# Block compression without paired columns, and the output gate of the delta-rule heads moved into the attention stage

## The chip, the cores and the metric

The kernel runs on one core of a Trainium2 chip. The metric is the device time of one execution in microseconds (us), where lower is better. The engines of the core are TensorE (PE; its weight loads are shown apart as PEld), VectorE (DVE), ScalarE (ACT), GpSimd (POOL) and SyncE (SP, which issues the DMAs). Each engine runs its own list of instructions in order and waits on semaphores that the others raise.

## What is computed

A decoder trunk of two layers on 512 tokens of width 1024, in float32. In each layer three groups of token mixers read the same normalised input: gated DeltaNet (4 heads of 64), sparse attention (8 query heads of 64 and 2 key/value heads, with a compressed, a selected and a window branch), and a short gated convolution. Then come an output projection and a SwiGLU feed-forward network. The change touches two parts of the reference:

```python
def compress_blocks(t, pe, w1, w2):
    nb = T // CMP_STRIDE                                   # 512 / 16
    blk = t.reshape(b, nb, CMP_STRIDE, g, d)
    win = jnp.concatenate([blk[:, :-1], blk[:, 1:]], axis=2) + pe[:, None, :]
    flat = win.transpose(0, 1, 3, 2, 4).reshape(b, nb - 1, g, CMP_LEN * d)
    return jax.nn.gelu(flat @ w1) @ w2                     # for keys and for values

o_gdn = rms_norm(o_gdn, gdn_norm[l]) * jax.nn.silu(heads(gz))
```

## The kernel before

**One layer on PE.** The input projection runs in 34 groups, numbered n = 0 to 33 (`GROUPS`); each is one PSUM bank filled in three passes (high and low parts of both operands, `three_pass`, L514). Other work is placed by hand between groups, by n, in the same order on every engine. After it come transposes of queries and keys, the attention stage, the output projection and the feed-forward network. The weights are fetched by SP, copied to `w_hi` by ACT (`split_hi`, L962), and `w_lo` is formed by POOL (`split_lo`, L1223).

**Compression.** Behind group 20 `cmp_first` (L553) multiplies `w1c` with the windows in `x2`: 32 float32 matmuls that the trace shows as 64 records. Those of the keys (k = 0) write PSUM partitions 0 to 63 and those of the values (k = 1) partitions 64 to 127, in turn, so that they use the two column halves of the array. The position term `pe` is not added to the data. It stands as two more window columns behind the 31 of each head (`NW1 = NC + 2`), copied into `x2` by ACT (L989). DVE's `cmp_hidden` (L1394 to L1403) adds it and does the GELU with a Tanh of ACT (L1046). Behind group 21 PE runs `cmp_second` (L563), DVE runs `cmp_norm` (L1407 to L1416, with the product of L1411), and behind group 23 PE runs `cmp_third` (L570).

**Gate of the delta-rule heads.** `z` holds the gate's input. At n = 9 ACT computes its Tanh (L1068), between the Tanh of beta (L1065) and the exponentials of the decay (L1069 to L1075), which DVE turns into `g` (L1451). PE's cumulative sum (L596) and POOL's `make_trig` wait for `g`. Later, between `one_minus(0)` (L1243) and `split_lo(10)`, POOL turns `z` into silu(z) times the norm gain (L1289, L1290, L1291) and raises `zgate`.

**Hops.** From n = 24 on, `hop` (L623, L662, L666) puts chains of dependent small matmuls between the passes. `hop_dve` and `hop_act` copy each result for the next one. DVE also normalises keys there (`k_norm`, L1503 and L1504, both inputs in SBUF).

**Attention.** 64 items (unit and query tile) run in ticks 0 to 75. In tick s: PE computes `scores(s)` (L754, L755), DVE its row maximum (L1682, L1679), ACT the exponential (L1135), DVE the reciprocal of the sum (L1688, in the next tick), and POOL scales the probabilities (`scale_probs`, L1315). PE transposes them three ticks later (`p_transpose(s)`, L771, in tick s + 3), DVE and ACT copy that to SBUF, and `pv` (L785) and `cmp_pv` (L793) follow. Two score tiles are issued together in each tick divisible by four. I call the scaling of item s scale(s) and its transposes ptr(s).

**The tail of the delta rule** lies in the same ticks, from OG_TICK = 41 on. ACT squares `og` (41), DVE sums (tick 42, L1720) and makes the inverse root by a seed and three Newton steps (tick 43, ten small operations, L1724 and L257 to L261). POOL has one piece per tick in ticks 45 to 52 ahead of its scaling: for each of four token tiles one product with the root (L1323) and one with the gate (L1326). PE transposes the two halves (`gdn_out`, L823) in ticks 54 and 56, and ACT and DVE split each into high and low (L977, L1729). The second of them waits until the first has been split.

Of the kernel before, what the change touches and what calls it, by code (L numbers as in the profile page):

```python
# [41 lines left out]
class Semaphores(dict):  # L42
# [22 lines left out]
    "norm_gains": 32, "oS": 4, "rb": 1, "rbps": 1, "rstd1": 1, "oall": 1, "og": 4, "ogT": 2, "ored": 1, "oroot": 1, "osq": 1, "pTa": 32, "pTd": 32,  # L65
# [4 lines left out]
    "x_res": 16, "zgate": 1, "zth": 1,  # L70
# [15 lines left out]
def trunk(nc, A, out):  # L86
# [7 lines left out]
    NW1 = NC + 2  # L94
# [31 lines left out]
    with ExitStack() as ctx:  # L126
        def sb(name, shape, dt=F32):
# [21 lines left out]
                      sb(f"kg{l}", [P, 3, HEAD]), sb(f"pe_c{l}", [P, 2, 16]), sb(f"w2c{l}", [P, HEAD]))  # L149
# [5 lines left out]
        peb = sb("peb", [P, 2])  # L155
# [34 lines left out]
        XW = T + CMP_LEN  # L190
        x2 = at(0, 2, 2, XW)
# [6 lines left out]
        hid = at(10240, 3, 2 * NC)  # L198
# [75 lines left out]
        def load_params(sp, l):  # L274
# [5 lines left out]
            def row(name, n):  # L280
# [4 lines left out]
                (p.w2c[:], A["nsa_cmp_w2"][l].rearrange("k i d -> (k i) d")),  # L285
# [180 lines left out]
        def tensor_layer(pe, l):  # L466
# [351 lines left out]
            def gdn_out(m):  # L818
                pe.wait_ge(*S.at("og", NT, l))
# [6 lines left out]
            for tick in range(N_ITEMS + LAG_PV):  # L826
# [14 lines left out]
                if tick in (OG_TICK + 13, OG_TICK + 15):  # L841
                    gdn_out((tick - OG_TICK - 13) // 2)
# [104 lines left out]
        def scalar_layer(act, l):  # L947
# [31 lines left out]
            def empty_group(n):  # L979
# [49 lines left out]
            for n in range(len(GROUPS)):  # L1029
# [33 lines left out]
                if n == 9:  # L1063
# [3 lines left out]
                    act.wait_ge(*S.at("gtr", 6, l))  # L1067
                    nc.scalar.activation(zt, z, ACT.Tanh, scale=0.5).then_inc(S["zth"], 1)  # L1068
# [80 lines left out]
            for tick in range(N_ITEMS + LAG_PV):  # L1149
# [24 lines left out]
                if tick in (OG_TICK + 14, OG_TICK + 16):  # L1174
                    m = (tick - OG_TICK - 14) // 2
# [38 lines left out]
        def pool_layer(pool, chain, l):  # L1214
# [38 lines left out]
            if l == 0:  # L1253
# [603 lines left out]
```

## Time and profile before

| | |
|---|---|
| median of 3 runs | 1549.39 us (1548.87 to 1550.99) |
| the profiled execution | 1548.87 us, its span 1546.8 us |
| PE busy | 1436.6 us, 93% of the span |
| DVE, POOL, ACT busy | 683.1, 645.1, 512.8 us |
| mean granted clock of PE | 0.971 of full speed |
| chain that ended last | PE 76%, DVE 13%, issue 4%, ACT 3%, POOL 2% |

The span is the time from the first to the last instruction; the execution's own time is 2.07 us longer. Times in rows count from the start of the span. The first layer's stages lie at about 29 to 226 us (input projection), 226 to 258 (queries and keys), 258 to 365 (attention) and 365 to 772 (output projection and feed-forward). The second layer repeats them about 768 us later. The clock is given as a share of full speed, so that 1.00 is 2.4 GHz and 0.5 is 1.2 GHz.

### The profile page before, as it was taken

The numbers are of one execution on the slowest core, as the hardware profiler recorded it, in microseconds if no ns is written. First come the engines' busy times: TensorE is split into PE (matmuls) and PEld (weight loads), VectorE is DVE, ScalarE is ACT, GpSimd is POOL, SyncE is SP. The second block draws the span as 40 slices with busy tenths as digits, with TensorE's granted clock in tenths as the row PEclk, the third lists the DMA queues.
The fourth block names the chain that finished last, engine by engine and source line by source line (L and its number), as shares of the span: only waits on it lengthen the run. The fifth ranks groups of instructions, "written<-read, shape, count | busy, mean of one in ns | idle before, by whom it ended". The sixth has DMA issues, their size and how long they took to land.

```text
span 1546.8 us, 19725 instructions
## 1 busy us (share of the span) xinstructions
PE 1436.6 (93%) x8050; PEld 1199.0 (78%) x8050; DVE 683.1 (44%) x1208; ACT 512.8 (33%) x888; POOL 645.1 (42%) x371
## 2 busy tenths in 40 slices
PE   5998986979999999999978989879799999999999
PEld 4887875647988888888868888756489888888887
DVE  6527467663334402433164284576623443033421
ACT  5453215452332312232235423154434232123220
POOL 4375332453343433434423833333433443443432
PEclk9999998999999999999989999979999999999999
DMA  6214120001533233233222341200022333333332
GB/s 170 85 57 106 50 55 1 1 1 44 98 84 108 77 102 109 82 109 93 84 76 64 80 105 28 55 1 1 1 56 82 106 85 102 101 84 109 83 101 75
DMA packets 182857, 112.64 MB, mean 73 GB/s; under 512 B 46576, under 2 KB 170480, under 8 KB 182768
## 3 DMA queue, kind: packets, MB, share of 16 engines
q1 hardware_dynamic: 182768, 111.39, 25.9%
q8 instruction: 64, 1.05, 0.3%
q14 instruction: 25, 0.20, 0.0%
HBM read 108.49 MB, written 2.88 MB: 72 GB/s over the span
## 4 chain that ended last, share of the span: by engine, by line
PE 76%; DVE 13%; issue 4%; ACT 3%; POOL 2%; DMA 1%; SPq 1%; ACTq 0%; DVEq 0%; POOLq 0%
PE ps L514 62%; PE ps L623 2%; PE ps L785 2%; PE ps L771 2%; DVE arena L1487 2%; DVE st L260 1%; DVE att L1682 1%; PE ps L754 1%; PE ps L755 1%; DVE arena L1495 1%; DVE hT_hi L1647 1%; DVE arena L271 1%; ACT hT_lo L977 1%; POOL w_lo L1223 1%; PE ps L469 1%
## 5 line engine op out<-in xcount | busy, mean ns | idle before, releaser
L1223 POOL TENSOR_TENSOR w_lo<-w_raw,w_hi 128x2048 fp32r<-128x2048 f32 (+1 forms) x100 | 453.5, 4535 | 628.9 <-ACT w_hi L962 628.9
L962 ACT ACTIVATE w_hi<-w_raw 128x2048 fp32r<-128x2048 f32 (+1 forms) x100 | 188.6, 1886 | 571.3 <-PE ps L514 570.9
L514 PE MATMUL ps<-hT_hi,w_lo 128*128 128x512 f32 x928 | 232.9, 393 | 0.0
L514 PE MATMUL ps<-hT_hi,w_hi 128*128 128x512 f32 x912 | 228.6, 392 | 0.4 <-DVE hT_lo L1364 0.4
L514 PE MATMUL ps<-hT_lo,w_hi 128*128 128x512 f32 x912 | 226.9, 390 | 0.0
L514 PEld LDWEIGHTS ps<-hT_hi,w_lo 128*128 128x128 f32 x928 | 175.6, 190 | 36.5
L514 PEld LDWEIGHTS ps<-hT_lo,w_hi 128*128 128x128 f32 x912 | 170.6, 188 | 35.6 <-issue 0.3
L514 PEld LDWEIGHTS ps<-hT_hi,w_hi 128*128 128x128 f32 x912 | 169.3, 188 | 36.2 <-DVE hT_lo L1364 1.3
L1729 DVE TENSOR_TENSOR aT_lo<-ffn_tmp,aT_hi 128x512 fp32r<-128x512 f32 x44 | 142.2, 3231 | 30.8 <-ACT aT_hi L977 30.8
L1784 DVE TENSOR_TENSOR ffn_tmp<-ps,ffn_tmp 128x512 f32<-128x512 f32 x44 | 30.4, 692 | 243.6 <-ACT ffn_tmp L1201 243.6
L514 PE MATMUL ps<-w_hi,aT_hi 128*128 128x512 f32 (+1 forms) x608 | 132.9, 345 | 0.0
L514 PE MATMUL ps<-w_lo,aT_hi 128*128 128x512 f32 (+1 forms) x608 | 132.3, 344 | 0.0
L514 PE MATMUL ps<-w_hi,aT_lo 128*128 128x512 f32 (+1 forms) x608 | 131.9, 344 | 0.0
L977 ACT ACTIVATE arena<-ps 128x512 f32<-128x512 f32 (+4 forms) x146 | 69.8, 494 | 179.1 <-PE ps L623 87.1
L514 PEld LDWEIGHTS ps<-w_hi,aT_hi 128*128 128x128 f32 x608 | 98.7, 188 | 15.4 <-issue 0.8
L514 PEld LDWEIGHTS ps<-w_hi,aT_lo 128*128 128x128 f32 x608 | 98.8, 188 | 14.5
L514 PEld LDWEIGHTS ps<-w_lo,aT_hi 128*128 128x128 f32 x608 | 98.8, 188 | 14.2
L1793 DVE SCALAR_TENSOR_TENSOR x_tok<-ps,st,x_tok 128x512 f32<-128x512 f32 x32 | 24.0, 750 | 189.1 <-PE ps L514 189.1
L623 PE MATMUL ps<-arena 128*128 128x128 f32 x512 | 71.7, 291 | 15.3 <-DVE arena L1552 6.9
L623 PEld LDWEIGHTS ps<-arena 128*128 128x128 f32 x512 | 65.4, 201 | 19.8 <-DVE arena L1552 7.8
L1315 POOL TENSOR_SCALAR arena<-arena,att,ngt 128x512 f32<-128x512 f32 (+3 forms) x80 | 51.5, 647 | 56.4 <-DVE att L1688 55.4
L754 PE MATMUL ps<-hT_lo,hT_hi 128*128 128x256 f32 (+2 forms) x128 | 58.2, 455 | 10.2 <-DVE hT_hi L1647 10.2
(283 smaller groups left out, 1836.6 us busy)
## 6 DMA issues: line engine op xcount, KB each, us to landing
w_raw<-in_w_gate_up SPq DMA_DIRECT2D x88, 512.0 KB, 5.1
w_raw<-in_w_in SPq DMA_DIRECT2D x20, 1024.0 KB, 5.4
w_raw<-in_w_down SPq DMA_DIRECT2D x16, 1024.0 KB, 5.1
w_raw<-in_w_out SPq DMA_DIRECT2D x32, 256.0 KB, 4.5
w_raw<-in_w_down SPq DMA_DIRECT2D x8, 768.0 KB, 4.5
w_raw<-in_w_in SPq DMA_DIRECT2D x2, 1120.0 KB, 5.8
w_raw<-in_w_in SPq DMA_DIRECT2D x2, 1056.0 KB, 6.3
x_tok<-in_x SPq DMA_DIRECT2D x4, 512.0 KB, 5.4
```

Of the source, the lines that this page charges most:

```text
L514: mm = nc.tensor.matmul(out_ap, a(ab, k), b(bb, k), start=first and i == 0, stop=last and i == len(kts) - 1)
L623: mm = nc.tensor.matmul(ps[:, bank, h * P:(h + 1) * P], lhs(h), rhs(h), start=True, stop=True)
L754: nc.tensor.matmul(o, q_ap, kst[:, br * 2 + g, 0:n], start=True, stop=False, skip_group_check=True)
L771: mm = nc.tensor.transpose(ps[:, 4 + s % 2, j * P:(j + 1) * P], prob[u % 2][i][:, j * P:(j + 1) * P], ident[:])
L785: nc.tensor.matmul(ps[rows, PV_BANK[p % 2], j * P:T], kv[:, j, v0:v0 + HEAD], pT[(2 * v + g) % 4][:, j * T:j * T + T - j * P], start=br == ...
L962: nc.scalar.activation(whi[:, c % 2, 0:kt * w], raw[:, c % 2, 0:kt * w], ACT.Copy).then_inc(S["w_hi"], 1)
L977: return nc.scalar.activation(dst, src, ACT.Copy)
L1223: nc.gpsimd.tensor_tensor(wlo[:, c % 2, 0:kt * w], raw[:, c % 2, 0:kt * w], whi[:, c % 2, 0:kt * w].bitcast(F32), ALU.subtract).then_inc(S ...
L1315: nc.gpsimd.tensor_scalar(prob[u % 2][i], prob[u % 2][i], att[:, 1, s % 8:s % 8 + 1], ngt[:, i, 3 * h + 1 + br:3 * h + 2 + br], ALU.mult, ...
L1487: chain(V.tensor_tensor(tmp, a, d, ALU.mult))
L1729: V.tensor_tensor(dst, full, hi.bitcast(F32), ALU.subtract).then_inc(done, 1)
L1784: V.tensor_tensor(ft[:, 2 + cnt % 2, :], ps[:, 2 * (i % 2) + 1, :], ft[:, cnt % 2, :], ALU.mult).then_inc(S["up_mul"], 1)
```

## The change

`cmp_first` no longer pairs keys with values. All its matmuls write partitions 0 to 63, first the 16 of the keys, then those of the values. The position term leaves `x2`. It is computed by 16 further matmuls for each k whose moving operand is one column of `pe_c`. `cmp_hidden` and `cmp_second` follow that layout: 64 partitions with keys and values side by side.

```diff
-                for m in range(16):
-                    for k in range(2):
-                        mm = nc.tensor.matmul(ps[k * HEAD:(k + 1) * HEAD, 3, 0:2 * NW1].rearrange("p (g n) -> p g n", g=2),
-                                              w1c[:, k, m, :], x2[:, k, :, 2 * m:2 * m + CMP_STRIDE * (NW1 - 1) + 1:CMP_STRIDE],
-                                              start=m == 0, stop=m == 15, skip_group_check=True)
+                for k in range(2):
+                    for m in range(16):
+                        nc.tensor.matmul(ps[0:HEAD, 3, k * P:k * P + 2 * NC].rearrange("p (g n) -> p g n", g=2),
+                                         w1c[:, k, m, :], x2[:, k, :, 2 * m:2 * m + CMP_STRIDE * (NC - 1) + 1:CMP_STRIDE],
+                                         start=(k == 0 and m == 0), stop=(m == 15), skip_group_check=True)
+                    for m in range(16):
+                        mm = nc.tensor.matmul(ps[0:HEAD, 3, k * P + 2 * NC:k * P + 2 * NC + 1], w1c[:, k, m, :],
+                                              prm[l].pe_c[:, k, m:m + 1], start=False, stop=(m == 15), skip_group_check=True)
...
-                    ev(x2[:, g, :, T:XW:2], prm[l].pe_c[:, g, :].rearrange("p (o m) -> p o m", o=1).broadcast_to([P, 2, 16]))
...
-                chain(V.tensor_copy(peb[:, 0:1], ps[:, 3, NW1 - 1:NW1]))
-                chain(V.tensor_scalar(hid[:, 0, :].rearrange("p (g n) -> p g n", g=2),
-                                      ps[:, 3, 0:2 * NW1].rearrange("p (g n) -> p g n", g=2)[:, :, 0:NC], peb[:, 0:1], None, ALU.add))
+                for k in range(2):
+                    chain(V.tensor_copy(peb[:, k:k + 1], ps[0:HEAD, 3, k * P + 2 * NC:k * P + 2 * NC + 1]))
+                for k in range(2):
+                    cols = slice(k * 2 * NC, (k + 1) * 2 * NC)
+                    chain(V.tensor_scalar(hid[:, 0, cols], ps[0:HEAD, 3, k * P:k * P + 2 * NC], peb[:, k:k + 1], None, ALU.add))
```

The gate's Tanh moves from n = 9 to tick 43 on ACT, and POOL's three gate operations leave the projection (with `zgate`, for which DVE waited at the groups of `cx`). In the attention POOL takes the Newton steps over from DVE, which keeps the seed. The pieces become 16 of 128x256, two per tick in ticks 44 to 47, one per tick in ticks 49 to 56, with a pass over `zt` in tick 48. `gdn_out` moves from ticks 54 and 56 to 58 and 60, and so do the splits of its results.

```diff
-                    act.wait_ge(*S.at("gtr", 6, l))
-                    nc.scalar.activation(zt, z, ACT.Tanh, scale=0.5).then_inc(S["zth"], 1)
...
+                if tick == OG_TICK + 2:
+                    act.wait_ge(*S.at("ored", 1, l))
+                    nc.scalar.activation(zt, z, ACT.Tanh, scale=0.5).then_inc(S["zth"], 1)
...
-            pool.wait_ge(*S.at("zth", 1, l))
-            chain(nc.gpsimd.tensor_scalar(zt, zt, 0.5, 0.5, ALU.mult, ALU.add))
-            chain(nc.gpsimd.tensor_tensor(z, z, zt, ALU.mult))
-            nc.gpsimd.tensor_tensor(z.rearrange("p t (h d) -> p (t h) d", d=HEAD), z.rearrange("p t (h d) -> p (t h) d", d=HEAD),
-                                    prm[l].gng[:].rearrange("p (o d) -> p o d", o=1).broadcast_to([P, NT * GH, HEAD]), ALU.mult
-                                    ).then_inc(S["zgate"], 1)
...
-                if tick == OG_TICK + 4:
-                    pool.wait_ge(*S.at("oroot", 1, l))
-                if OG_TICK + 4 <= tick < OG_TICK + 12:
-                    gdn_piece(tick - OG_TICK - 4)
+                if tick == OG_TICK + 2:
+                    pool.wait_ge(*S.at("oseed", 1, l))
+                    newton(st[:, 2, 0:16], st[:, 1, 0:16], st[:, 3, 0:16])
+                if OG_TICK + 3 <= tick < OG_TICK + 7:
+                    gdn_piece(2 * (tick - OG_TICK - 3))
+                    gdn_piece(2 * (tick - OG_TICK - 3) + 1)
+                if tick == OG_TICK + 7:
+                    pool.wait_ge(*S.at("zth", 1, l))
+                    chain(nc.gpsimd.tensor_scalar(zt, zt, 0.5, 0.5, ALU.mult, ALU.add))
+                if OG_TICK + 8 <= tick < OG_TICK + 16:
+                    gdn_piece(tick - OG_TICK)
                 scale_probs(tick)
...
-                    rsqrt(chain, st[:, 2, 0:16], st[:, 1, 0:16], st[:, 3, 0:16])
-                    dve.nop().then_inc(S["oroot"], 1)
+                    V.tensor_scalar(st[:, 2, 0:16].bitcast(I32), st[:, 1, 0:16].bitcast(I32), -0.5, RSQRT_SEED,
+                                    ALU.mult, ALU.add).then_inc(S["oseed"], 1)
...
-                if tick in (OG_TICK + 13, OG_TICK + 15):
-                    gdn_out((tick - OG_TICK - 13) // 2)
+                if tick in (OG_TICK + 17, OG_TICK + 19):
+                    gdn_out((tick - OG_TICK - 17) // 2)
```

## Rows read from the trace of the kernel before

**Rows 1.** The page: busy time, share of the span and instructions.

```profile
PE 1436.6 (93%) x8050; PEld 1199.0 (78%) x8050; DVE 683.1 (44%) x1208; ACT 512.8 (33%) x888; POOL 645.1 (42%) x371
```

**Rows 2.** Windows: length, busy (instructions) of PE, PEld, DVE, ACT, POOL; clock, DMA, GB/s.

```profile
325.00:344.00 19.00, 13.57 (x84) 9.01 (x84) 13.23 (x38) 9.55 (x36) 12.78 (x21) 0.91 0.00 1
...
365.00:772.00 407.00, 406.79 (x1992) 343.84 (x1991) 129.26 (x117) 108.76 (x110) 165.34 (x38) 1.00 0.34 94
...
346.00:350.10 4.10, 4.10 (x13) 1.10 (x11) 0.16 (x1) 1.15 (x5) 1.19 (x2) 0.58 0.00 0
```

**Rows 3.** Timeline at the decay's exponentials: start, length, engine, line, operation, [wait before].

```profile
75.44 1.04 ACT L1068 ACTIVATE arena<-arena 128x1024 f32<-128x1024 f32 x1
76.50 1.28 ACT L1069 ACT_TABLE_LOAD   x1
...
80.11 0.40 PE L596 MATMUL ps<-gsc,tri 128*128 128x16 f32 x2 [4.00 <-DVE gsc L1451]
```

**Rows 4.** Timeline at the compression.

```profile
130.35 4.07 PE L553 MATMUL ps<-arena 128*64 128x66 f32 x64
...
140.27 0.22 DVE L1399 TENSOR_TENSOR arena<-arena 128x62 f32<-128x62 f32 x1
...
141.33 0.42 PE L563 MATMUL ps<-w2c,arena 64*31 64x64 f32 x8 [1.24 <-DVE arena L1403]
...
142.67 4.62 POOL L1223 TENSOR_TENSOR w_lo<-w_raw,w_hi 128x2048 fp32r<-128x2048 f32 x1 [9.04 <-ACT w_hi L962]
143.11 4.32 DVE L1411 TENSOR_TENSOR arena<-arena 31x128 f32<-31x128 f32 x1
...
150.33 0.24 PE L570 MATMUL ps<-ident,arena 31*128 31x31 f32 x1 [2.64 <-DVE arena L1416]
```

**Rows 5.** Timeline: two short float32 batches of a hop on PE.

```profile
169.12 1.10 PE L662 MATMUL ps<-arena 128*128 128x64 f32 x8 [0.87 <-ACT arena L977]
...
170.16 0.66 PE L666 MATMUL ps<-arena 128*64 128x128 f32 x8
```

**Rows 6.** Timeline at POOL's gate operations, among the hops.

```profile
159.45 1.49 POOL L1289 TENSOR_SCALAR arena<-arena 128x1024 f32<-128x1024 f32 x1
...
160.06 1.42 DVE L1504 TENSOR_TENSOR arena<-arena,kg 128x512 f32<-128x512 f32 x1
...
161.02 2.68 POOL L1290 TENSOR_TENSOR arena<-arena 128x1024 f32<-128x1024 f32 x1
...
162.25 1.16 PE L623 MATMUL ps<-arena 128*128 128x128 f32 x8 [1.27 <-DVE arena L1550]
...
166.74 0.69 DVE L1504 TENSOR_TENSOR arena<-arena,kg 128x512 f32<-128x512 f32 x1
```

**Rows 7.** Timeline: POOL's Newton steps for the queries, first and last of 12 operations.

```profile
204.13 0.24 POOL L1247 TENSOR_TENSOR st<-st 128x32 f32<-128x32 f32 x1
...
207.66 0.25 POOL L1250 TENSOR_TENSOR st<-st 128x32 f32<-128x32 f32 x1
```

**Rows 8.** Timeline of POOL in the attention: scale(42), two pieces, scale(56).

```profile
324.56 0.66 POOL L1315 TENSOR_SCALAR pbuf<-pbuf,att,ngt 128x384 f32<-128x384 f32 x1 [1.83 <-DVE att L1688]
...
329.08 0.61 POOL L1323 TENSOR_TENSOR arena<-arena,st 128x256 f32<-128x256 f32 x1
...
330.32 0.73 POOL L1326 TENSOR_TENSOR arena<-arena 128x256 f32<-128x256 f32 x1
...
346.79 0.45 POOL L1315 TENSOR_SCALAR pbuf<-pbuf,att,ngt 128x128 f32<-128x128 f32 x1
```

**Rows 9.** Timeline of PE in the attention: ptr(43), second gdn_out, ptr(53), ptr(57).

```profile
328.75 0.66 PE L771 MATMUL ps<-ident,arena 128*128 128x128 f32 x4 [2.29 <-POOL arena L1315]
...
345.43 0.63 PE L823 MATMUL ps<-ident,arena 128*128 128x128 f32 x4 [2.34 <-DVE aT_lo L1729]
345.89 0.38 PE L771 MATMUL ps<-ident,arena 128*128 128x128 f32 x2
...
353.74 0.41 PE L771 MATMUL ps<-ident,pbuf 128*128 128x128 f32 x2 [0.88 <-POOL pbuf L1315]
```

More of the change, by code:

```diff
@@ L64 @@
     "mix_lo": 4, "mixc_hi": 2, "mixc_lo": 2, "mixg_hi": 2, "mixg_lo": 2, "mm": 142, "ngth": 1, "nmax": 48,
[L65 removed]
+    "norm_gains": 32, "oS": 4, "rb": 1, "rbps": 1, "rstd1": 1, "oall": 1, "og": 1, "ogT": 2, "ored": 1, "oseed": 1, "osq": 1, "pTa": 32, "pTd": 32,
     "params": 160, "pscaled": 64, "ptr": 64, "pv": 64, "qdec": 1, "qhi": 8, "qkmask": 1, "qkn": 1, "qlo": 4, "qn": 1,
@@ L69 @@
     "vbs": 1, "vnew": 4, "w1": 32, "wS": 4, "w_hi": 50, "w_in0": 656, "w_in1": 656, "w_lo": 50, "x_down": 16,
-    "x_res": 16, "zgate": 1, "zth": 1,
+    "x_res": 16, "zth": 1,
 }
@@ L148, in trunk @@
                       sb(f"alog{l}", [P, GH]), sb(f"dtb{l}", [P, GH]), sb(f"gng{l}", [P, HEAD]), sb(f"qg{l}", [P, HEAD]),
-                      sb(f"kg{l}", [P, 3, HEAD]), sb(f"pe_c{l}", [P, 2, 16]), sb(f"w2c{l}", [P, HEAD]))
+                      sb(f"kg{l}", [P, 3, HEAD]), sb(f"pe_c{l}", [P, 2, 16]), sb(f"w2c{l}", [HEAD, 2, HEAD]))
                for l in range(DEPTH)]
@@ L154, in trunk @@
         ngt = sb("ngt", [P, NT, 3 * NH])
-        peb = sb("peb", [P, 2])
+        peb = sb("peb", [HEAD, 2])
         vcr = sb("vcr", [P, P])
@@ L189, in trunk @@
         L = at(6144, NT * GH, P)
-        XW = T + CMP_LEN
-        x2 = at(0, 2, 2, XW)
+        x2 = at(0, 2, 2, T)
         qd = at(6144, NT, GW)
@@ L197, in trunk @@
         w1c = at(3072, 2, 16, HEAD)
-        hid = at(10240, 3, 2 * NC)
+        hid = at(10240, 3, 2 * 2 * NC)[0:HEAD]
         kcn = at(10240 + 12 * NC, 2, P)[0:32]
@@ L284, in load_params @@
             params += [
-                (p.w2c[:], A["nsa_cmp_w2"][l].rearrange("k i d -> (k i) d")),
+                (p.w2c[:], A["nsa_cmp_w2"][l].rearrange("k i d -> i k d")),
                 (p.scw[:, 0], A["conv_w"][l].rearrange("k (j p) -> j p k", p=P)[0]),
@@ L561, in cmp_second @@
                     for g in range(NG):
-                        rows = slice(k * HEAD, (k + 1) * HEAD)
-                        mm = nc.tensor.matmul(ps[0:NC, (7, 3)[k], g * HEAD:(g + 1) * HEAD],
-                                              hid[rows, 0, g * NC:(g + 1) * NC], prm[l].w2c[rows, :],
+                        mm = nc.tensor.matmul(ps[0:NC, 7, (k * 2 + g) * HEAD:(k * 2 + g + 1) * HEAD],
+                                              hid[:, 0, k * 2 * NC + g * NC:k * 2 * NC + (g + 1) * NC], prm[l].w2c[:, k, :],
                                               start=True, stop=True)
@@ L818, in gdn_out @@
             def gdn_out(m):
-                pe.wait_ge(*S.at("og", NT, l))
+                pe.wait_ge(*S.at("og", 1, l))
                 if m == 1:
@@ L987, in empty_group @@
                         act.wait_ge(*S.at("gback", 4, l))
-                        act.wait_ge(*S.at("params", 16 * (N_PARAMS - 6), l))
-                    ev(x2[:, g, :, T:XW:2], prm[l].pe_c[:, g, :].rearrange("p (o m) -> p o m", o=1).broadcast_to([P, 2, 16]))
                     for gg in range(2):
                         rows = slice(gg * HEAD, (gg + 1) * HEAD)
-                        ev(x2[0:HEAD, g, gg, 0:T], b[rows, :])
+                        ev(x2[0:HEAD, g, gg, :], b[rows, :])
                         i = ev(x2[HEAD:P, g, gg, 0:T - 1], b[rows, 1:T])
@@ L1173, in scalar_layer @@
                     ev(ahi[:, 6 + m, :], ccb[:, m, :]).then_inc(S["mixc_hi"], 1)
-                if tick in (OG_TICK + 14, OG_TICK + 16):
-                    m = (tick - OG_TICK - 14) // 2
+                if tick in (OG_TICK + 18, OG_TICK + 20):
+                    m = (tick - OG_TICK - 18) // 2
                     act.wait_ge(*S.at("ogT", m + 1, l))
@@ L1319, in gdn_piece @@
             def gdn_piece(k):
-                t, a = divmod(k, 2)
+                a, t = divmod(k, NT)
                 heads = slice(t * GH, (t + 1) * GH)
                 if a == 0:
-                    chain(nc.gpsimd.tensor_tensor(o3[:, heads], o3[:, heads], st[:, 2, heads].rearrange("p (n o) -> p n o", o=1)
-                                                  .broadcast_to([P, GH, HEAD]), ALU.mult))
-                else:
-                    nc.gpsimd.tensor_tensor(og[:, t], og[:, t], z[:, t], ALU.mult).then_inc(S["og"], 1)
+                    i = nc.gpsimd.tensor_tensor(o3[:, heads], o3[:, heads], st[:, 2, heads].rearrange("p (n o) -> p n o", o=1)
+                                                .broadcast_to([P, GH, HEAD]), ALU.mult)
+                elif a == 1:
+                    i = nc.gpsimd.tensor_tensor(o3[:, heads], o3[:, heads], prm[l].gng[:].rearrange("p (o d) -> p o d", o=1)
+                                                .broadcast_to([P, GH, HEAD]), ALU.mult)
+                elif a == 2:
+                    i = nc.gpsimd.tensor_tensor(zt[:, t], zt[:, t], z[:, t], ALU.mult)
+                else:
+                    i = nc.gpsimd.tensor_tensor(og[:, t], og[:, t], zt[:, t], ALU.mult)
+                if k < 15:
+                    chain(i)
+                else:
+                    i.then_inc(S["og"], 1)
             for tick in range(N_ITEMS):
@@ L1409, in cmp_norm @@
                     cols = slice(b % 2 * HEAD, (b % 2 + 1) * HEAD)
-                    chain(V.tensor_copy(vcr[32 * b:32 * b + NC, cols], ps[0:NC, 3, cols]))
+                    chain(V.tensor_copy(vcr[32 * b:32 * b + NC, cols], ps[0:NC, 7, P + b % 2 * HEAD:P + (b % 2 + 1) * HEAD]))
                 chain(V.tensor_tensor(kcn[0:NC, 1, :], kcn[0:NC, 0, :], kcn[0:NC, 0, :], ALU.mult))
@@ L1756, in vector_layer @@
                     lo_part(alo[:, MIX_LO[6 + m], :], ccb[:, m, :], ahi[:, 6 + m, :], S["mixc_lo"])
-                if tick in (OG_TICK + 14, OG_TICK + 16):
-                    m = (tick - OG_TICK - 14) // 2
+                if tick in (OG_TICK + 18, OG_TICK + 20):
+                    m = (tick - OG_TICK - 18) // 2
                     dve.wait_ge(*S.at("mixg_hi", m + 1, l))
```

2 lines of the change are left out of this document (removed).

## Prediction

> **What bounds the kernel now.** I read the page first. PE is busy for 93% of the span and no other engine for half [rows 1]. Then the table by windows. The feed-forward stretch is full at full clock and holds nothing that the change touches [rows 2], so the answer lies in the stages where PE waits for chains of small work. There the reader should look at what ends PE's waits: the exponentials of the decay [rows 3], the compression and the DMA-and-DVE work around it [rows 4], the hops [rows 6], and in the attention POOL's scalings and the split behind the first `gdn_out` [rows 9]. POOL is busy 12.8 of 19 us in ticks 43 to 53 [rows 2]. It looks free on average, but the ptr that PE waits for is the one POOL has just scaled.
>
> **The change part by part, for one layer.**
>
> *Tanh off the chain of the decay.* The Tanh takes 1.04 us on ACT, directly ahead of a table load and the exponentials [rows 3]. PE waits 4.00 us for what comes of them, so the whole 1.04 is on the path: **-1.04 us**. It could be 0 if something else were as late, and no more than 1.04. The same Tanh comes back in tick 43, in the tables of the attention's exponentials. There it lies beside POOL's Newton steps. If it needed tables of its own, two loads of 1.28 us would come on top, still beside POOL.
>
> *Compression.* The 64 records take 4.07 us, 0.064 each [rows 4]. The order without pairs keeps the 64 and adds 64 with one column. A short batch can't go faster than its weight loads: L662, with 128 weight columns and 64 moving ones, takes 1.10 us for 8 records, and L666, with 64 weight columns, 0.66 us [rows 5]. That puts a record with 64 weight columns between about 0.03 (a one-column record that overlaps its load) and 0.11. I take 0.063, which is nearest to the same weights in L553, so PE's part grows by 4.0 us (1.9 to 3.8 and more below, under the rivals, above). Two DVE operations more and three of double width make `cmp_u` later by about 0.66 us: two of 0.2 to 0.3 as L1399, and 0.2 for the width.
>
> What hides it: PE waits 1.24 us ahead of L563 and 2.64 us ahead of L570 [rows 4]. Group 21 would end at 141.33 - 1.24 + 4.0 = 144.1, `cmp_second` at 144.5. The next two groups took 6.0 us (from 141.75 to 150.33 - 2.64), so they end at 150.5, while L570 can't start before 150.33 as it is. DVE has its copies done by 145.9. Then comes L1411: 31x128 in 4.32 us, ending at 147.43, 0.14 us behind POOL's L1223. It did not compute for 4.32 us. It stood until POOL was done. POOL's pass follows ACT's `split_hi`, which stands behind the Tanh of `cmp_u`, so it comes 0.66 later and L1411 ends at 148.1. The 2.9 us from there to L570 stay. L570 starts at 151.0: **+0.67 us**. The 4 us on PE are worth next to nothing as long as that cover of 2.5 + 2.6 us holds.
>
> By the Trainium skill, "TensorEngine Tiling (Array Packing)", Instruction Overhead, a matmul with one column costs as much as one with 60, an overhead of about 60 cycles. By that page the 64 short ones would be an estimated 1.6 us at 2.4 GHz, and the net would be the same +0.67, since it hangs on POOL.
>
> *Gate operations off POOL among the hops.* Nobody waits for them, and `split_lo(10)` waits for ACT anyway. But DVE's L1504, both inputs in SBUF, takes 1.42 us beside L1289 and 0.69 us when POOL is at nothing that lasts [rows 6]. PE then waits 1.27 us for the next copy of DVE. With POOL empty DVE is 0.73 earlier: **-0.73 us** (0 to -1.27). This trace shows the same in L1411. The Trainium skill, "SBUF — State Buffer", Who interferes with whom, has the rule: a DVE `tensor_tensor` with two SBUF inputs and a GpSimd operation exclude each other for a whole instruction, and this trace agrees.
>
> *Attention.* After tick 42 POOL is the pacer. scale(42) ends at 325.22 [rows 8]. Then, in POOL's order:
> - Newton steps: 12 operations took 3.78 us for 32 columns [rows 7]; for 16 columns 3.7.
> - scale(43) to scale(56): 0.45 us for 128 columns, 0.66 for 384 [rows 8], about 0.105 per 128 columns: three rounds of 2.43, with 0.77 and 0.45, 8.5.
> - 16 pieces, each waited for before the next (0.08 gap): 8 as L1323 (0.61 + 0.08), 8 as L1326 (0.73 + 0.08): 12.0.
> - the pass over `zt` as L1289, 1.49 + 0.08: 1.6.
>
> The sum is 25.8 us: scale(56) ends at 351.0, where it ended at 347.24 before. That is 3.8 later. Not all of it reaches PE. Before, scale(43) waited for DVE, which made the root itself (wait of 2.29 us at ptr(43) [rows 9]); that time is POOL's now, and ptr(43) goes from 328.75 to about 329.8. ptr(53) comes at 346.8, three pieces and three scalings short of 351.0, against 345.89: +0.9. From ptr(53) to ptr(57) PE took 353.74 - 345.89 = 7.85 us. Out of that go 0.88 of waiting [rows 9] and the slow clock: the 4.1 us at 0.58 would be 2.4 at full clock [rows 2]. In come both `gdn_out` (0.46 each), the wait for the split between them, which stands in the same place of the tick order (2.34), and 0.3 for `og`, whose last piece is done at 350.5. 7.85 - 0.88 - 1.7 + 0.92 + 2.34 + 0.3 = 8.8, so ptr(57) is at 355.6, against 353.74: +1.9. The stretch at 0.58 began 0.6 us behind the end of that wait. After the moved one I expect most of the 1.7 back: +1.3. Attention: **+3.2 us** (0 to 6).
>
> What is queued behind the new waits: behind POOL's wait for the seed and its steps stands scale(43), and for it PE's ptr(43), all later scores and everything on DVE and ACT that reads them. Behind `og` stands PE's ptr(55).
>
> *Sum.* -1.04 + 0.67 - 0.73 + 3.2 = +2.1 us per layer, +4.2 for two. The profiled execution took 1548.87 us, 0.5 less than the median, so 1553.1 on its scale and **1553.6 us** on the median's.
>
> **The rivals.**
>
> *The attention hides all of it (faster).* Over many ticks PE, DVE and ACT may be slower than POOL, so that POOL's lag is made up before tick 58, and the stall at tick 43 disappears with DVE's ten small operations. For it: POOL is idle for 6 of 19 us in this stretch. Against it: 25.8 us of work are more than the 22.0 between the same points before. It decides where scale(53) ends no later than 345.8. Attention 0: -1.1 per layer, 1549.4 - 2.2 = 1547.2 us.
>
> *Half of it is hidden (no change).* POOL's lag is repaid but for about 1.5 us: +0.4 per layer, 1550.2 us.
>
> *The unpaired columns are slow.* If a weight load can't run under the matmul before it in the same column half, or the strided windows stream slowly, the first 64 records cost 0.11 us each (the pitch of L662) and the others 0.06: 10.8 us for 4.07, +6.7. Group 21 ends at 146.8, and two groups later L570 starts at 153.3, 3.0 later and not 0.67. Against it: L666 has such loads too and takes 0.08 per record. +2.3 per layer: 1558.2 us. The Trainium skill, "TensorE: Matmul & The Clock Gate", Part 3, has a rule of this kind: weight loads overlap running matmuls only where the row group differs.
>
> *The clock stays low.* POOL's pace leaves PE gaps in ticks 43 to 57, and each stretch such as that of 4.1 us at 0.58 costs 1.7 us [rows 2]. One more per layer: 1557.0 us.
>
> **How the numbers follow.** Forecast 0.40, hidden 0.14, half hidden 0.20, slow columns 0.14, low clock 0.12. The range of 8 in 10 runs from 1548.5 to 1561 us: it leaves out most of the hidden case (about 0.1) and the slow columns together with a low clock or an attention at its upper bound (about 0.1). The forecast alone is 1552 to 1556. 0.2% is 3.1 us, about what a measurement can tell from no change; up to 1552.5 counts as the same. Faster: 0.14. Same: the half-hidden case and the lower edge of the forecast, 0.22. Slower: 0.64.
>
> **What would show it.** In the changed profile, PE's cumulative sum starts about 1 us earlier. The compression has 128 records in about 8 us, and its transpose starts 0.4 us earlier than before (-1.04 + 0.67). The first waits 2.64 shrink to about 0.5. DVE's second product of the first `k_norm` takes 0.7 us. POOL has no gap over 0.5 us from scale(42) to scale(56), and PE's waits name POOL. The second `gdn_out` waits over 2 us in tick 60. The forecast is wrong if POOL shows gaps there, if the unpaired matmuls take more than 9 us, or if PE's waits in ticks 57 to 75 vanish.

## The result, and the profile after

| | before | after |
|---|---|---|
| median of the timed runs | 1550.19 us (1548.87 to 1552.54) | 1569.49 us (1563.86 to 1570.02) |
| ratio, 95% interval | | 1.0102 (1.0084 to 1.012) |
| profiled execution, span | 1548.87, 1546.8 us | 1563.39, 1561.6 us |

The change makes the kernel about 1% slower: 13 to 19 us by the interval, 19.3 by the medians, where 4.2 were forecast. The time lies above the whole range. Where it went in the profiled execution (+14.5 us) is read in three places. First comes the compression, by the timeline of after (start, length, engine, line, operation, in brackets the wait before and who ended it):

```profile
128.56 3.62 PE L551 MATMUL ps<-arena 128*64 128x62 f32 x32
...
132.00 1.99 PE L555 MATMUL ps<-pe_c,arena 128*64 128x1 f32 x32
...
133.86 3.59 PE L551 MATMUL ps<-arena 128*64 128x62 f32 x32
...
137.27 2.11 PE L555 MATMUL ps<-pe_c,arena 128*64 128x1 f32 x32
...
139.42 0.33 DVE L1404 COPY peb<-ps 64x1 f32<-64x1 f32 x2 [1.95 <-PE ps L555]
...
145.00 0.63 PE L563 MATMUL ps<-w2c,arena 64*31 64x64 f32 x8
145.16 1.91 ACT L962 ACTIVATE w_hi<-w_raw 128x2048 fp32r<-128x2048 f32 x1 [3.57 <-PE ps L512]
...
147.16 4.62 POOL L1222 TENSOR_TENSOR w_lo<-w_raw,w_hi 128x2048 fp32r<-128x2048 f32 x1 [15.34 <-ACT w_hi L962]
147.59 4.20 DVE L1424 TENSOR_SCALAR st<-st 31x2 f32<-31x2 f32 x1
...
154.19 0.24 PE L570 MATMUL ps<-ident,arena 31*128 31x31 f32 x1 [2.63 <-DVE arena L1427]
```

The 128 records take 10.8 us (128.56 to 139.38), where 64 took 4.07 [rows 4]. From start to start, a record with 62 columns costs (132.00 - 128.56) / 32 = 0.107 us, one with a single column (133.86 - 132.00) / 32 = 0.058. PE's wait before L563 is gone. The one before L570 is still 2.63, although everything ahead of it is later. From the first record to L570 it is 25.63 us against 19.98 [rows 4]: **+5.65 us**, and +5.8 in the second layer (903.05 to 928.82 against 897.02 to 917.01).

Second come the small terms, by the timeline: the cumulative sum, the second product of the first `k_norm`, the hop behind it, and L662.

```profile
78.38 0.40 PE L596 MATMUL ps<-gsc,tri 128*128 128x16 f32 x2 [3.03 <-DVE gsc L1462]
...
163.92 0.69 DVE L1515 TENSOR_TENSOR arena<-arena,kg 128x512 f32<-128x512 f32 x1
...
165.39 1.16 PE L623 MATMUL ps<-arena 128*128 128x128 f32 x8 [0.55 <-DVE arena L1561]
...
172.25 1.10 PE L662 MATMUL ps<-arena 128*128 128x64 f32 x8 [0.87 <-ACT arena L977]
```

The wait of 4.00 [rows 3] is 3.03: tanh gives back 0.97. L1515 takes 0.69 where the same operation (L1504 of before) took 1.42, and PE waits 0.55 and not 1.27 [rows 6]. From L570 to L662 it is 18.06 us against 18.79 [rows 4, 5]: -0.73, the forecast's figure. In the second layer it is 18.06 against 19.88: 0.71 of that is the same wait (1.26, now 0.55), the rest a longer stretch at a low clock in the execution of before.

Third comes the attention. From the first record of ptr(42) to the end of ptr(63) it is 39.8 us (328.75 to 368.52) against 35.25 (325.51 to 360.76): **+4.5 us**; in the second layer 39.7 against 34.7. The second `gdn_out` still has its wait, and behind it the slow clock, 4.1 us at 0.58, the same as [rows 2]:

```profile
358.89 0.63 PE L823 MATMUL ps<-ident,arena 128*128 128x128 f32 x4 [2.33 <-DVE aT_lo L1739]
```

```profile
358.90:363.00 4.10, 4.10 (x18) 2.22 (x19) 0.68 (x3) 1.78 (x6) 1.20 (x2) 0.58 0.00 0
```

-0.97 + 5.7 - 0.73 + 4.5 is +8.5 per layer, +17 for two. The profiled execution shows 14.5; some of the rest is the start (the first matmul comes 0.8 us earlier, which the change has no part in) and stretches at a low clock that differ between executions.

### The profile page after: what moved, and what is told of

Same layout as the page of the kernel before. It is cut to its first block, busy times and chain, and to the rows that moved or that the text cites. A ratio compares the mean times of both kernels' runs of the same rounds, so it can differ in the third digit from the quotient of the medians.

```text
span 1561.6 us, 20009 instructions
## 1 busy us (share of the span) xinstructions
PE 1452.0 (93%) x8178; PEld 1213.9 (78%) x8178; DVE 679.0 (43%) x1194; ACT 513.0 (33%) x884; POOL 651.0 (42%) x407
## 4 chain that ended last, share of the span: by engine, by line
PE 79%; DVE 9%; POOL 4%; issue 4%; ACT 3%; DMA 0%; SPq 0%; POOLq 0%; ACTq 0%; DVEq 0%
PE ps L512 64%; PE ps L623 2%; PE ps L785 2%; PE ps L771 2%; POOL arena L1308 1%; PE ps L551 1%; DVE st L258 1%; DVE att L1692 1%; DVE arena L1506 1%; PE ps L754 1%; DVE hT_hi L1657 1%; DVE arena L269 1%; PE ps L755 1%; ACT hT_lo L977 1%; POOL w_lo L1222 1%
## 5 line engine op out<-in xcount | busy, mean ns | idle before, releaser
L512 PEld LDWEIGHTS ps<-w_hi,aT_lo 128*128 128x128 f32 x608 | 98.8, 188 | 14.5
```

Of the source, the lines that this page charges most:

```text
L512: mm = nc.tensor.matmul(out_ap, a(ab, k), b(bb, k), start=first and i == 0, stop=last and i == len(kts) - 1)
```

## The experiments

Each kernel is compared with runs of the kernel before on the same chip, whose medians were 1551.26 us (for e1 to e4), 1550.62 (e5 to e8), 1551.17 (e9 to e11) and 1550.35 (e12).

**e1_comp_only and e2_gates_only: the two halves of the change.** Each is the kernel before with one half of the diff shown above: e1 has the hunks on `cmp_first`, `cmp_second`, `cmp_hidden`, `peb`, `w2c`, `hid`, `x2`; e2 all others.

> The kernel before with the compression part of the change alone (unpaired records, one-column records, five hidden-layer operations, the new layout). Theory from the trace of after: the first matmuls of the compression take 10.8 us per layer in place of 4.07, the compression's transpose starts 5 to 6 us later, and most of that reaches the end: +9 to +11 us over the kernel before. Rival, the forecast as put on record: +0.67 us per layer, +1.3 us, because PE's wait before the second product and the cover behind it hide the matmuls. Second rival: the timed runs of after were some 5 us above its profiled one at a slightly lower clock; if that belongs to the compression, this kernel comes out at +14 or more.

> The kernel before with the gate part of the change alone (tanh, gate operations, Newton steps on POOL, gdn_out four ticks later). Theory from the trace of after: tanh off the decay chain -1.0, free DVE among the hops -0.7, attention +4.7, sum +2.9 per layer, +5 to +6 us. The forecast on record: -1.04 - 0.73 + 3.2 = +1.4 per layer, +2.9 us. Rival: attention hides all of it, -1.8 per layer, -3.5 us. scale(56) should end 3.8 us (forecast) or 4.2 us (trace of after) later, measured from ptr(42), than in the kernel before.

Measured: e1 1563.48 us (1559.41 to 1564.81, 5 runs), ratio 1.0078 (1.0064 to 1.0092), **+12.2 us**. e2 1556.47 us (1553.39 to 1557.63), ratio 1.0032 (1.0019 to 1.0044), **+5.2 us**. The halves add up: 17.4, inside the interval of the whole. The forecast had +1.3 and +2.9. So e1's miss is 11 us, e2's 2.3: the compression is where the prediction broke. The theories drawn from the trace of after expected 9 to 11 and 5 to 6.

e1's profiled execution shows more than the records' price. Timeline of its second layer, and windows (length, busy of PE, PEld, DVE, ACT, POOL, clock):

```profile
912.66 3.49 PE L555 MATMUL ps<-pe_c,arena 128*64 128x1 f32 x32
916.09 3.78 PE L512 MATMUL ps<-hT_hi,w_hi 128*128 128x512 f32 x8
```

```profile
904.00:909.20 5.20, 5.20 (x65) 5.20 (x64) 4.92 (x9) 0.60 (x1) 3.22 (x2) 1.00 0.00 0
...
912.60:916.20 3.60, 3.60 (x36) 3.59 (x34) 0.26 (x2) 0.00 (x0) 0.00 (x0) 0.50 0.24 77
916.20:920.00 3.80, 3.80 (x9) 3.02 (x10) 2.11 (x9) 0.31 (x1) 0.00 (x0) 0.50 0.28 26
```

Behind the first 32 one-column records (907.40 to 909.25) the granted clock falls: 0.64 in the next window, 0.50 (1.2 GHz) in the two behind it, although PE has work without a gap. The second 32 then take 3.49 us (1.99 at full clock), and the group behind them 3.78 for eight records that take 2.11 at full clock.

**e3_swap_loops: pairing alone.**

```diff
-for m in range(16):
-    for k in range(2):
+for k in range(2):
+    for m in range(16):
         mm = nc.tensor.matmul(ps[k * HEAD:(k + 1) * HEAD, 3, 0:2 * NW1]...
```

> The kernel before with only the two loops around the 64 records of the compression exchanged, so that records of the same column half follow each other; no one-column records, nothing else changed. If a record's time is that of its moving columns (66 columns at 0.11 us) and the pairs of before ran side by side in two column halves, the 64 records take 6.9 to 7.1 us in place of 4.07. Rival, the forecast: 0.064 each either way, 4.1 us. On the whole: +2.9 us on PE are partly hidden by the wait before the second product (1.24) and by the cover of 2.5 us behind: 0 to +2 per layer, 0 to +4 us; if the clash of DVE and POOL moves with it, up to +3 per layer.

Measured: 1553.97 us (1552.08 to 1554.71, 11 runs), ratio 1.0017 (1.0008 to 1.0026), +2.7 us. The timeline:

```profile
130.91 7.04 PE L553 MATMUL ps<-arena 128*64 128x66 f32 x64
...
143.55 0.42 PE L563 MATMUL ps<-w2c,arena 64*31 64x64 f32 x8
...
145.72 4.61 POOL L1223 TENSOR_TENSOR w_lo<-w_raw,w_hi 128x2048 fp32r<-128x2048 f32 x1 [11.54 <-ACT w_hi L962]
145.96 4.38 DVE L1413 TENSOR_SCALAR st<-st 31x2 f32<-31x2 f32 x1
...
152.74 0.24 PE L570 MATMUL ps<-ident,arena 31*128 31x31 f32 x1 [2.83 <-DVE arena L1416]
```

The order of two loops costs 7.04 - 4.07 = 2.97 us on PE. From the first record to L570 it is 21.83 us, +1.85, so only 1.1 of the 2.97 are absorbed (the next section says where). The wait before L570 covers nothing of it: it is 2.83 where it was 2.64.

**e5_no_one_col: the one-column records taken away.** e1 without the second loop over `m`; the position bias is left out of the result (`peb` is copied from column 0).

> The compression part alone, without the 32 one-column matmuls (64 records), so the position bias is left out of the result; everything else as in e1_comp_only. Theory: 64 unpaired records at 0.107 are 6.9 us (+2.8), and the transpose comes 2.8 - 1.24 + 0.2 = 1.8 later than before, plus 0.7 of DVE, +2 to +2.5 us per layer: 1555.5 to 1556.5 us. The one-column records are also what lets the granted clock fall: without them the window of the compression and the group behind it stays at 1.00, and the timed runs lie within 2.5 us of each other, where e1_comp_only had 1559.4 and 1563.1 to 1564.8. Rival: the clock falls here as well, from the unpaired 64-column weights alone; then 1560 and a spread of 4 to 5 us.

Measured: 1554.09 us (1553.23 to 1555.04, 11 runs), ratio 1.0020 (1.0011 to 1.0029), **+3.5 us**, a spread of 1.8. The median lies a little under the 1555.5 to 1556.5 that were expected, the spread is as expected. The clock in the window of the records and the group behind:

```profile
130.80:138.00 7.20, 7.20 (x66) 6.98 (x66) 6.76 (x13) 0.60 (x1) 3.32 (x2) 1.00 0.01 2
138.00:145.00 7.00, 7.00 (x39) 5.66 (x40) 4.43 (x17) 1.64 (x2) 0.00 (x0) 1.00 0.22 48
```

Without the one-column records the clock stays at 1.00 there, as it does in e3. The 64 one-column records are therefore worth 12.2 - 3.5 = 8.7 us, 4.35 per layer: 3.8 are their own time (10.82 - 7.05). The 0.5 that are left would be the clock that falls behind them, but the medians can't show that: the intervals of e1 and e5 are each over 1 us to either side. The profiled executions show it, and that it varies: from the first record to L570 e1 takes 27.2 and 29.0 us, that of after 25.6 and 25.8.

**e6_widths: what a record's time hangs on.** e1 with other moving operands. The matmuls that read `pe_c` take one column for k = 0 and 16 side by side for k = 1.

```diff
-x2[:, k, :, 2 * m:2 * m + CMP_STRIDE * (NC - 1) + 1:CMP_STRIDE]   # both k, 62 columns
+x2[:, k, :, 2 * m:2 * m + NC]                                     # k = 0, 62 side by side
+x2[:, :, :, 2 * m:2 * m + CMP_STRIDE * (NC - 1) + 1:CMP_STRIDE]   # k = 1, 124, 16 apart
```

> The compression part alone with other moving operands, so the result is not the reference's: k=0 reads 62 columns that lie side by side, k=1 reads 124 columns 16 elements apart, then one column (k=0) and 16 columns side by side (k=1). Three theories for the 0.107 us of an unpaired record with 62 columns. Weight load and matmul one after the other: 62 side by side cost the same 0.107, 124 cost 0.16, 16 columns 0.07. The reading of columns 16 elements apart: 62 side by side fall to the 0.058 of a one-column record, 124 cost 0.21, 16 columns 0.058. A fixed time per unpaired record above some width: 0.107 for all three wide forms.

One run (1562.16 us), read by its profile alone: the timeline, and the window over the 124-column records:

```profile
130.08 2.08 PE L552 MATMUL ps<-arena 128*64 128x62 f32 x32
...
132.00 1.98 PE L561 MATMUL ps<-pe_c,arena 128*64 128x1 f32 x32
...
133.84 6.91 PE L556 MATMUL ps<-arena 128*64 128x124 f32 x32
...
140.57 2.00 PE L561 MATMUL ps<-pe_c,arena 128*64 128x16 f32 x32
```

```profile
134.00:140.60 6.60, 6.60 (x33) 5.54 (x33) 5.07 (x14) 0.00 (x0) 0.00 (x0) 0.74 0.03 10
```

From start to start, 62 columns side by side cost (132.00 - 130.08) / 32 = 0.060 us, one column (133.84 - 132.00) / 32 = 0.058, 124 columns 16 elements apart (140.57 - 133.84) / 32 = 0.210; in after, 62 of these cost (132.00 - 128.56) / 32 = 0.107. 16 side by side are as one. The second theory holds, the others fall: a weight load that can't run under its matmul would make 62 side by side as slow. The spread-out columns cost 1.7 ns each, and that doesn't follow PE's clock: the 124-column records stay 0.21 us apart all through this window, in which the clock is 1.00, then 0.50, then 1.00 again (mean 0.74), and the second 62-column run of after, at 0.53, takes 3.59 us where the first, at 1.00, took 3.62. In the kernel before two such streams ran in turn, one for each column half, at 0.127 per pair [rows 4]. e3 has the same 64 records without the alternation at 0.109 each, 0.218 for two. So two strided streams overlap when they alternate between the halves.

**e7_comp_unlocked and e8_late_unlocked: POOL's pass moved out of the way.**

```diff
+pool.wait_ge(*S.at("hop_dve", 1, l))
 split_lo(9)
 one_minus(0)
```

in e1, and in e4_tanh_late (below).

> The compression part alone, and POOL's pass for chunk 9 of the weights waits for the second copy of the hops, so that it no longer runs while DVE works on the compression's keys. Theory: the 2.63 us that PE waits before the compression's transpose are the lock of DVE behind that pass, which itself follows the end of group 21; without it the wait falls from 2.63 to under 0.5 and the kernel is 2 to 2.6 us per layer faster than e1_comp_only, 4 to 5 us in all: 1558.5 to 1559.5. Rival: DVE's chain needs that time anyway (the wait stays above 2) or the hops wait for the moved pass in its place: no change, 1563.5.

> The kernel of e4_tanh_late (no unpaired columns, tanh late) with the same wait before POOL's pass for chunk 9. Theory as for e7_comp_unlocked: the wait of 2.64 us before the transpose falls below 0.5; 4 to 5 us under e4_tanh_late, 1543 to 1544. Rival: no change, 1548.

Measured: e7 1564.09 us (1562.15 to 1565.11, 4 runs), e8 1548.41 us (1544.62 to 1551.57, 11 runs): no gain over e1 (1563.48) and e4 (1547.99). The timeline of e8 says why:

```profile
146.45 0.24 PE L570 MATMUL ps<-ident,arena 31*128 31x31 f32 x1
...
149.75 2.02 PE L623 MATMUL ps<-arena 128*128 128x128 f32 x16 [1.91 <-DMA arena<-diag_out]
...
152.65 4.54 POOL L1223 TENSOR_TENSOR w_lo<-w_raw,w_hi 128x2048 fp32r<-128x2048 f32 x1 [20.18 <-DVE arena L1547]
...
155.32 2.42 DVE L1504 TENSOR_TENSOR arena<-arena,st 128x512 f32<-128x512 f32 x1
...
157.78 1.63 DVE L1505 TENSOR_TENSOR arena<-arena,kg 128x512 f32<-128x512 f32 x1
...
160.19 1.16 PE L623 MATMUL ps<-arena 128*128 128x128 f32 x8 [2.62 <-DVE arena L1551]
```

The first half of the theory is shown: without POOL's pass beside it DVE's chain is short and L570 starts with no wait, 3.0 us earlier than in e4, of which 0.3 are there at L563 already (in e7 it has no wait either). But the 3.0 are given back at once. 1.91 go to the DMA that brings the diagonal blocks, 1.35 more to the hop behind the product that now stands beside the moved pass (wait 2.62, [rows 6] had 1.27). At the end of the hops 0.6 us are left (231.81 against 232.41 in e4). My expectation of 4 to 5 us was wrong; the rival is what happened.

**e4_tanh_late: tanh alone.**

```diff
 n == 9:   -nc.scalar.activation(zt, z, ACT.Tanh, scale=0.5).then_inc(S["zth"], 1)
 n == 23:  +nc.scalar.activation(zt, z, ACT.Tanh, scale=0.5).then_inc(S["zth"], 1)  # behind the squares
```

> The kernel before with only the gate's Tanh moved from ahead of the exponentials of the decay to behind the two squares of the k_norm in group 23, where ACT waits 5 us; POOL's gate operations stay between the hops, and start only later. The forecast's first term says -1.04 us per layer, -2.1 us. Rival: something else is as late, 0. In the trace the cumulative sum should start 1.0 us earlier, and so should the compression's first record.

Measured: 1547.99 us (1544.61 to 1549.94, 11 runs), ratio 0.9977 (0.9968 to 0.9985), **-3.3 us**. The wait at the cumulative sum is 3.04, and the Tanh takes its 1.04 us where ACT has nothing else:

```profile
78.07 0.61 PE L596 MATMUL ps<-gsc,tri 128*128 128x16 f32 x2 [3.04 <-DVE gsc L1451]
...
148.30 1.04 ACT L1103 ACTIVATE arena<-arena 128x1024 f32<-128x1024 f32 x1
```

The rows account for 1.9 of the 3.3; the interval (2.3 to 5.0) begins just above that, so what the rest is stays open. One profiled execution is a poor judge of 1 us here: behind the wait at L596 stands a stretch at a low clock that is longer in one layer than in the other. From L596 to the compression's first record it is 51.39 and 50.21 us in e4's two layers, 50.24 and 51.50 in those of before. That takes back the gain at the first record of e4's first layer.

**e9_newton_dve: the Newton steps.** e2 with `rsqrt` back on DVE and no `newton` on POOL.

> The gate part alone (as e2_gates_only), with the root's Newton steps back on DVE; the moved tanh and the 16 pieces stay. Theory: POOL is the pacer from tick 43, so its 3.6 us less show in full in the end of scale(56), and at ptr(43) the wait falls from 3.15 back to about 2.3; PE gains 0.9 there and up to 1.3 by ptr(57), but not the clock lost behind the second gdn_out: 1 to 1.5 us per layer, 2 to 3 us under e2_gates_only (1556.5), 1553.5 to 1554.5. Rival: the pieces pace it anyway, or DVE's ten steps cost what POOL's did: within 1 us of e2_gates_only.

Measured: 1553.46 us (1552.03 to 1555.02, 11 runs), ratio 1.0016 (1.0007 to 1.0025), 3.0 us under e2, as expected, though the two intervals overlap. In the trace ptr(43) waits 2.36 us in place of 3.15. From ptr(42) to the end of ptr(63) e9 takes 37.57 and 38.53 us in its two layers, where e2 takes 39.44 and 39.23. So Newton on POOL is worth 0.7 in the second layer. In the first it is 1.9, but 1.2 of them lie behind ptr(57): there the second `gdn_out` waits 2.34 us as ever, and the clock stays at 1.00 behind it, where the second layer has 0.59. e2 lost 5.2 in all and gained some 3.4 ahead of the attention, so the attention costs it about 8.6 (4.2 + 4.5 in its trace). Without Newton on POOL, e9 still takes 2.3 and 3.8 longer there than the kernel before, which leaves the pieces and the pass over `zt` as the greater part. How much of the 3.0 is Newton and how much is the clock stays open.

POOL's chain in e2 itself, by the timeline: scale(42), first and last Newton step, scale(43), scale(56):

```profile
323.09 0.66 POOL L1310 TENSOR_SCALAR pbuf<-pbuf,att,ngt 128x384 f32<-128x384 f32 x1 [1.83 <-DVE att L1698]
323.72 0.22 POOL L1248 TENSOR_TENSOR st<-st 128x16 f32<-128x16 f32 x1
...
326.99 0.22 POOL L1251 TENSOR_TENSOR st<-st 128x16 f32<-128x16 f32 x1
327.32 0.77 POOL L1310 TENSOR_SCALAR arena<-arena,att,ngt 128x512 f32<-128x512 f32 x1
...
349.37 0.45 POOL L1310 TENSOR_SCALAR pbuf<-pbuf,att,ngt 128x128 f32<-128x128 f32 x1
```

**e10_spacing, e11_late_spacing, e12_gates_spaced: the wait between the two `gdn_out`.**

```diff
-if tick in (OG_TICK + 13, OG_TICK + 15):      # e12: + 17, + 19
-    gdn_out((tick - OG_TICK - 13) // 2)
+if tick in (OG_TICK + 13, OG_TICK + 17):      # e12: + 17, + 21
+    gdn_out((tick - OG_TICK - 13) // 4)
```

with ACT's and DVE's halves of the split moved likewise.

> The kernel before with only the second gdn_out moved from tick 56 to tick 58, and ACT's and DVE's halves of its split with it. In the trace of before PE waits 2.34 us for the split between the two, and runs at 0.6 of the clock for some 4 us behind that wait. Theory: a wait of this length is what lets the clock fall; with other work between the two both the 2.34 and the 1.7 us of slow clock go, up to 4 us per layer, of which the next wait takes some back: -2 to -7 us. Rival: the wait stands two ticks later at the same price and so does the slow clock, as in e2_gates_only: 0.

> e4_tanh_late and e10_spacing together. They touch different stages, so their gains should add: e4_tanh_late gave -3.3 us, so 3.3 us under whatever e10_spacing gives. Rival: the gain of the one is taken back in the other's stage, no better than e4_tanh_late.

> The gate part alone (e2_gates_only) with the second gdn_out at tick 62 in place of 60, and its split with it. Theory: of the 4.2 us per layer that the attention costs in e2_gates_only, the wait of 2.34 us behind the first gdn_out and the slow clock behind it are not new, they stood in the kernel before too, but they now come as late as everything else; spacing removes both here as in e10_spacing (-5.8 us in all): 1550 to 1552. Rival: at tick 62 the split is so close to the out-projection that the wait appears there: within 1.5 us of e2_gates_only (1556.5).

Measured: e10 1545.39 us (1542.85 to 1546.65, 5 runs), ratio 0.9962 (0.9950 to 0.9975), **-5.8 us**. e11 1542.00 us (1538.28 to 1545.08, 5 runs), ratio 0.9949 (0.9935 to 0.9962), **-9.2 us**, 3.4 below e10: the gains add. e12 1554.55 us (1550.83 to 1558.85, 12 runs), ratio 1.0030 (1.0017 to 1.0044): not told apart from e2, and not the 1550 to 1552 that I expected. The timeline of e10, and the window behind its first `gdn_out`:

```profile
343.19 0.66 PE L823 MATMUL ps<-ident,arena 128*128 128x128 f32 x4 [0.92 <-POOL arena L1326]
...
348.84 0.61 PE L823 MATMUL ps<-ident,arena 128*128 128x128 f32 x4
...
356.34 0.66 PE L771 MATMUL ps<-ident,arena 128*128 128x128 f32 x4 [1.69 <-POOL arena L1315]
```

```profile
346.00:350.00 4.00, 4.00 (x25) 2.17 (x25) 2.00 (x5) 2.65 (x10) 1.65 (x3) 1.00 0.00 0
```

The second `gdn_out` no longer waits, and the clock stays at 1.00 where [rows 2] had 0.58. A wait of 1.69 later takes a part back. In e12 PE ends ptr(63) 2.0 us sooner than in e2, but in the first layer a slow stretch comes at the very end, behind two waits (1.52 and 0.88 us). In the second layer the clock is 1.00 there (1134 to 1138). The window of the first layer:

```profile
362.40:366.30 3.90, 3.90 (x10) 1.30 (x10) 0.00 (x0) 0.00 (x0) 3.40 (x1) 0.50 0.00 0
```

## Why the prediction was wrong, step by step

- **Compression, +0.67: the step that failed, in two places.** *The price.* "I take 0.063, which is nearest to the same weights in L553" made 4.0 us more on PE; it was 6.75. The one-column records cost 0.058 each, near the 0.063 of the sum. What was mis-sized are the 64 records with windows, which the sum left at 4.07: the 0.064 of L553 [rows 4] is half the time of a pair. Without pairs, windows 16 elements apart cost 0.107 (after) to 0.109 (e3, e5), 6.9 to 7.0 us for the 64, and the reading, not the weights, sets it (e6). The Trainium skill has the rule that I missed ("SBUF — State Buffer", section on Door 1, "SBUF cachelines"): an access that leaves its 16-byte line pays, so float32 strides are free up to 4. e6 agrees: 0.060 against 0.107 for the same 62 columns. By the Trainium skill ("TensorEngine Tiling (Array Packing)", Instruction Overhead) the 64 short ones would be an estimated 1.6 us; 3.9 were measured from start to start. That one column costs as much as some 60 agrees with e6, as long as the columns lie side by side (0.058 and 0.060).
- *The cover.* "The 4 us on PE are worth next to nothing as long as that cover of 2.5 + 2.6 us holds." Of PE's delay only 1.1 us were absorbed, and not by PE's own waits. I hung L570 on POOL's pass, the pass on ACT's `split_hi(9)`, and that on the Tanh. But `split_hi(9)` also waits for the end of group 21, whose weights lie in the buffer that it writes. Before, group 21 ended at 141.33 - 1.24 = 140.09 [rows 4], 0.6 before `split_hi(9)` started, so what stands directly ahead of it in the timeline of before is the Tanh (L1046). Its last records on PE, and the two operations of ACT:

```profile
138.11 1.97 PE L514 MATMUL ps<-hT_hi,w_lo 128*128 128x512 f32 x8
...
140.53 0.26 ACT L1046 ACTIVATE arena<-arena 128x62 f32<-128x62 f32 x1 [9.47 <-DVE arena L1399]
140.69 1.90 ACT L962 ACTIVATE w_hi<-w_raw 128x2048 fp32r<-128x2048 f32 x1
```

  After, group 21 ends at 145.07 (its last records in the timeline of after):

```profile
143.09 1.97 PE L512 MATMUL ps<-hT_hi,w_lo 128*128 128x512 f32 x8
```

  `split_hi(9)` starts at 145.16, then POOL at 147.16, DVE is free at 151.79, L570 starts at 154.19: PE's delay comes back to PE through three engines. Counted from the first record, `split_hi(9)` and POOL start 6.3 us later than before, 0.5 less than PE's delay. L570 starts another 0.6 less late, since DVE is stopped further on in its chain (3.04 us from POOL's end to L570 before, 2.41 after). e3 shows the path alone: 2.97 on PE, the same 0.5 and 0.6 off, 1.85 at L570. With my own price this path would have given 4.0 - 1.1 = +2.9. So of the miss of 5.0 per layer, 2.2 are the path and 2.8 the price.
- *The clock*, no term of the compression: it falls behind the one-column records (e1), and without them it doesn't (e5). Its part in e1's 6.1 per layer is too small for the medians to tell; in e1's profiled execution it is 1.6 and 3.2 us over that of after.
- That DVE stands behind POOL was right. Which operation it is changed with the shift: not the product of L1411, but a `tensor_scalar` on 31x2 stands 4.20 us. e8, where it takes 0.16, shows that POOL's pass is the cause. The Trainium skill ("SBUF — State Buffer", Who interferes with whom) lists `tensor_scalar` among the operations that can take the shared pair; this trace agrees.
- **Tanh, -1.04:** right in the trace (-0.97, and 3.04 in e4).
- **Gate operations off the hops, -0.73:** right to the digit in the first layer, by the wait that was named.
- **Attention, +3.2: right mechanism, 1.0 to 1.8 too small** (4.2 and 4.5 in e2's two layers, 4.5 and 5.0 in after's). Set on the forecast's scale (1.47 later, the lag at ptr(42)), e2 has ptr(43) at 329.6 (forecast 329.8), the end of scale(56) at 351.3 (351.0), ptr(53) at 347.2 (346.8), ptr(57) at 356.1 (355.6). POOL was the pacer with no gap. Half of the miss in e2's first layer is ahead of ptr(57) (356.1 for 355.6). The other half is the clock: for the slow stretch behind ptr(57) I charged 1.3. It moved with the wait, and ptr(57) to ptr(63) takes 1.8 longer (8.15 us against 6.37).
- **The rivals.** "The unpaired columns are slow" had 0.11, 0.06 and 10.8 us, at a chance of 0.14. In part that is luck: its 0.11 was called the pitch of L662, whose rows give (170.16 - 169.12) / 8 = 0.13 [rows 5], and of its two conditions only the slow reading holds. It still came out at 1558.2, because its delay of 3.0 at L570 leaned on the same cover. "Against it: L666 has such loads too" was the wrong row: its moving columns lie side by side, and its records alternate between the column halves. The hidden cases fall: scale(53) ends at 347.1 on that scale, 1.3 behind its deciding point. "The clock stays low" came true in part, and at a lower price than its 1.7: in the second layer of after and of e2 a third slow stretch stands behind a wait of 1.72 us at ptr(47) (1117 to 1121 us in after, 1109 to 1113 in e2; the same wait of 1.71 in e2's first layer has none behind it), and in the first layer of after the one behind ptr(43) runs on to 339 us. In e2 the second layer, with it, costs 4.5, the first, without it, 4.2, so most of it is absorbed where PE waits for POOL anyway.
- **Open.** Of the four timed runs of after three lie near 1569.5 us and one at 1563.9; of e1's five, four at 1563.1 to 1564.8 and one at 1559.4. e5's eleven lie within 1.8. That this is the clock in and behind the one-column records fits e1's rows, but the execution profiled of after is of the lower group (its 0.5 stretch ends with the second wide records), so for the upper one it is argued and not shown.

## What to carry to other kernels

A wait is cover only if what ends it doesn't itself start from the work that you lengthen: follow each semaphore of the releasing chain back in the code, also those that the profile doesn't name because they came second by half a microsecond. Two matmul streams with slow reads can overlap when they alternate between column halves (4.07 us for 64 records, 7.04 without), so take the price of an unpaired one from a record that reads at the same stride, not from half a pair. And before moving work, look at waits of PE of two microseconds that stand alone: spacing the two `gdn_out` by two ticks gave more (5.8 us) than anything that the change set out to move, and with tanh late 9.2. It has to be measured in place, though: in e12, where they stand later, the same spacing gave nothing that the runs can tell.

## What the runs showed of the hardware

- Columns 64 bytes apart reach PE at 1.7 ns each (0.107 / 62, 0.210 / 124), whatever its clock; side by side, 1, 16 and 62 columns cost the same 0.058 to 0.060 us per record at full clock. One-column records take (916.09 - 912.66) / 32 = 0.107 at 0.50, so these do follow the clock.
- The clock fell to 0.50 in a stretch where PE was busy without a gap, behind one-column records (e1, 913 to 920 us); without these it stayed at 1.00 (e5). It fell to 0.58 behind PE's wait of 2.34 us before the second `gdn_out`, and stayed at 1.00 without that wait (e10). The wait alone doesn't decide it: in e9's first layer the same 2.34 us were followed by 1.00.
- A DVE operation on 31x2 elements stood for 4.2 us beside POOL's pass, and took 0.16 us when the pass was moved away (e8).
